# Key and query splits stored by the front, and per-pair near scores of the sample on three column tiles, in a hybrid attention, RG-LRU and HGRN2 layer

## The chip, the cores and the metric

One core of a Trainium2 chip runs the whole program in one launch. The metric is the device time of that launch in microseconds (us). Engines are named as in the profile: PE is the matmul engine (PEld its weight loads), DVE the vector engine, ACT the scalar engine, POOL GpSimd, SP the engine whose queue issues every DMA here.

## The reference, cut to what matters

One layer is applied to a prompt of 2048 positions and to a sample group of 8 sequences with 8 new tokens each, all in f32. After an RMSNorm the input is multiplied by `w_in` (1024 x 4608); the columns feed three head groups, whose gated outputs are multiplied by `w_out`, added to the input and normed.

- Group A (6 heads of 64) is dilated attention. For the prompt each query looks at keys at distance up to 128, at every 4th key up to 512 and at every 16th up to 2048; the three branches are merged by their softmax denominators:

```
scores = einsum('bthd,btnhd->bthn', q, kg) * dh ** -0.5
p = exp(scores - max); o = einsum('bthn,btnhd->bthd', p, vg) / sum(p)
out = sum_over_branches(softmax(lse) * o) * silu(g_A)
```

- For the sample the same three branches run over a cache of 2048 keys per sequence and the 8 new ones.
- Group B is a gated linear recurrence (RG-LRU) after a convolution, group C a chunked matrix recurrence (HGRN2).

Products that matter for precision are made of a high and a low part of each operand: x_hi is x rounded to fp32r, x_lo = x - x_hi, and the kernel adds two or three products of such parts.

## The kernel before, in words

The program has two blocks, with a barrier of all engines between them.

**front** (L266 to L1295) makes the projections. `front_schedule` (L155) returns one list of steps; every engine walks the same list and does its part of each step, so the list sets the order on each queue. A step `("p", ci, g)` is the product of one group of 128 columns with one of five column blocks of the tokens (512, 384, 384, 384, 448 wide; the last holds the 64 sample tokens): 24 matmuls into one of three PSUM banks. PE may start product i when product i - 3 has been read (`bank_free`, L1195). `FORDER` has the column groups: 6 for group B, then 3 of keys ("k"), then for each of 6 HGRN heads f, c and one of q0, q1, q2, a0, a1, a2. From there on each product is cut into a half step `"e"` and a half step `"p"`, and after each half a few steps of the HGRN recurrence run.

- Keys (ACT, L716 to L726): ACT copies the bank into `kf`, sorted by position modulo 4 ("by class"), and SP stores the whole of one key group, 128 rows of 8448 bytes, to `zf` in DRAM after its fifth product (L439). A step `"k"` turns `kf` with PE, copies on DVE and stores `k_win_prompt`.
- Queries (ACT, L708): the bank goes by class to `stage[0]`, and SP stores it to `zf` in pieces of 384 bytes (L430).
- SP walks the same list: the store of a product is issued at the next `"p"` step (`before`, L473 on).

**attend_project** (L1496 on) has the attention over the prompt and, interleaved in its first part, the products of the values and the sample's HGRN part; then the output product with the sample's attention between its steps. `attend_schedule` (L1401) returns its list.

- Each head has 32 units `"u"`. In a unit PE makes the scores of 128 queries against up to 512 keys as two matmuls (L2495 with `khi`, L2496 with `klo`) into one of three banks; the moving operand is `qst`, which holds query_hi in partitions 0 to 63 and query_lo in 64 to 127, with the key parts on both halves. DVE adds a mask and takes the row minimum (L2267), ACT takes the exponential (L2115). Later steps `"t"` turn four blocks of probabilities (L2563), copy them out of PSUM (L1634 on ACT, L1636 on DVE), and `"o"` multiplies them with the values (L2586). The `"t"` of head h begin 11 units into head h + 1. Before the first of them POOL scales all probabilities of the head in ten operations (L2021), when the branch weights are there.
- The split of keys and queries: raw keys and queries come from `zf` in 4 parts per head (two of keys, two of queries), twice each, for both partition halves (L1799, 8 DMAs of 256 KB per head). ACT rounds each part (L2072, step `"s"`), DVE subtracts (L2252 for keys, L2256 for queries, step `"sd"`), and for queries ACT copies the result into tile order as `qn` (L2077, step `"se"`). `khi`, `klo` have two buffers; `qst` and `qn` have one, so the last query part of a head is made at units 4, 6 and 8 of that head, the rest at units 12 to 26 of the head before.
- PE waits for the key split at the first unit of a head and for `q_near` at units 0 and 16 (L2484 on).

The sample's attention (steps `"sr"`, `"ss"`, `"sk"`, `"sc"`, `"sx"`, `"sn"`, `"sm"`, `"so"`, `"sb"`, one sequence b at a time) stands between the half tiles `"pp"` of the output product, each of which is 27 matmuls of 512 columns (L49 to L51). In `"sk"` PE turns the 512 near keys for three head pairs (L2451), and makes the near scores of all 6 heads as three accumulating products of 512 columns (L2456): `qbd` holds, for each pair, the 48 query rows of all heads with zeros in the rows of the other pairs, so output rows are 48 and each product adds one pair. The scores of the 8 new keys (L2462) and of the far keys (L2468) go to the same bank. The probabilities are then turned (L2611, L2612, L2616), and `"so"` multiplies with the values on three column tiles, 16 rows in each (L2630).

Of the kernel before, what the change touches and what calls it, by code (L numbers as in the profile page):

```python
# [110 lines left out]
FCOL = {"q": 0, "k": 384, "a": 1152, "x": 1536, "g": 1920, "c": 2304, "f": 3072}  # L111
ZROW = {"q": ZQ, "k": ZK, "a": ZGA, "c": ZQC, "f": ZFC}
# [153 lines left out]
def front(nc, sem, io, con, zf, zt, mab, mt):  # L266
# [7 lines left out]
    with ExitStack() as ctx:  # L274
        end = ROOM + 4 * FREE

        def sb(name, shape, dt=F32):
# [68 lines left out]
                 "fs_store", "st_store", "const", "held")  # L346
# [13 lines left out]
        stages, stored, z_count, kinds = {}, [0] * NR, {}, {}  # L360
        for s in made:
            kind = kinds[s] = "t" if s[0] == "t" else FORDER[s[1]][0]
            if s[0] == "t" or kind in "qa":
                r = 0 if s[0] == "p" else (len(stages) + (s[1] == 2)) % NR
                stages[s] = r, stored[r]
                stored[r] += 2 if kind == "q" and s[2] == NFG - 1 else 1
# [3 lines left out]
        gate_stores = [max(stages[("t", 1, j)][1] + 1 for j in range(XTILES) if stages[("t", 1, j)][0] == r) for r in range(NR)]  # L370
        by_class = lambda t: t.rearrange("p (g i) -> p g i", g=NC)
# [24 lines left out]
        def _(sp):  # L396
# [14 lines left out]
            def store(s):  # L411
# [12 lines left out]
                if kind == "q":  # L424
                    r = stages[s][0]
                    m = min(n, SEQ - t0)
                    rows = slice((ZQ + c) * P, (ZQ + c + 1) * P)
                    sp.wait_ge(S["z_out"], BASE + z_count[s])
                    dst = by_class(zf[rows, 0:SEQ])[:, :, t0 // NC:(t0 + m) // NC]
                    sp.dma_start(dst, by_class(stage[r][:, :m])).then_inc(z_store[r], 16)  # L430
                    if m < n:
                        sp.dma_start(zf[rows, SEQ:T], stage[r][:, m:n]).then_inc(z_store[r], 16)
# [40 lines left out]
            before = None  # L473
            for s in sched:
                kind, a, b = s
                if kind == "r" and a + NX < XTILES:
# [165 lines left out]
        def _(act):  # L642
# [39 lines left out]
            def out(s):  # L682
# [20 lines left out]
                if kind in "qa":  # L703
# [3 lines left out]
                    if kind == "q":  # L707
                        ins = A(by_class(stage[r][:, :m]), in_turn(src[:, :m]), ACT.Copy)  # L708
# [6 lines left out]
                elif kind == "k":  # L715
# [7 lines left out]
                    ins = A(by_class(kf[c % 2][:, 0:SEQ])[:, :, t0 // NC:(t0 + m) // NC], in_turn(src[:, :m]), ACT.Copy)  # L723
                    if m < n:
                        ins = A(kf[c % 2][:, SEQ:T], src[:, m:n], ACT.Copy)
# [2024 lines left out]
```

## Time and profile before

| | |
|---|---|
| runs | 1743.97, 1744.19, 1745.74 us; median 1744.19 |
| the profiled execution | 1739.62 us, of which the trace spans 1737.9 |
| PE busy | 1606.0 us, 92% |
| DVE, ACT, POOL busy | 1012.0, 844.6, 628.4 us |
| DMA | 162.69 MB, mean 94 GB/s |

The front takes the first 1079 us or so of the span, the attention over the prompt ends near 1420, the rest is the output product with the sample's attention. A time in the rows below is counted from the start of the span. A PE row's duration is modelled and overlaps with the next; the distance from one start to the next is what an instruction takes in a row of them. "Idle before" and the releaser name what an engine waited for.

### The profile page before, as it was taken

How to read it: one execution, taken by the hardware profiler on the slowest of the kernel's cores; microseconds unless marked ns; L12 is line 12 of the kernel's file. 1: busy time of each engine (PE TensorE's matmuls, PEld its weight loads, DVE VectorE, ACT ScalarE, POOL GpSimd, SP SyncE). 2: the span in 40 equal slices, each digit the busy share in tenths (PEclk: the TensorE clock that was granted, in tenths of full speed). 3: DMA queues.
4: the chain of work that ended last, by engine and by line, in shares of the span. 5: the costliest groups of instructions: out<-in, count | busy, mean ns of one | idle time of the engine just before them, and what ended most of it. 6: DMA issues, size and time to landing. Idle time of an engine off the chain costs nothing. (4 is left out here: it accounts for less than half of the span.)

```text
span 1737.9 us, 38458 instructions
## 1 busy us (share of the span) xinstructions
PE 1606.0 (92%) x15345; PEld 1343.2 (77%) x15345; DVE 1012.0 (58%) x2044; ACT 844.6 (49%) x1620; POOL 628.4 (36%) x745
## 2 busy tenths in 40 slices
PE   6999997999999999999999998798888988999998
PEld 5988986989888888888787877785666666767775
DVE  3437655322366777677776764348776556565552
ACT  4427874211355555666667772545777631111120
POOL 1002220200366766666666663114444621212110
PEclk9999998999999999999999999897999889999999
DMA  6311011113212121121212112437651175676651
GB/s 209 108 50 40 21 44 56 57 58 125 76 30 65 30 63 29 42 55 32 66 27 64 32 38 74 121 90 173 169 134 50 62 223 166 195 236 186 225 168 52
DMA packets 182703, 162.69 MB, mean 94 GB/s; under 512 B 65571, under 2 KB 169022, under 8 KB 182142
## 3 DMA queue, kind: packets, MB, share of 16 engines
q1 hardware_dynamic: 182526, 160.24, 31.2%
q8 instruction: 122, 2.00, 0.5%
q14 instruction: 55, 0.45, 0.1%
HBM read 116.89 MB, written 46.55 MB: 94 GB/s over the span
## 5 line engine op out<-in xcount | busy, mean ns | idle before, releaser
L49 PE MATMUL f_bank<-c_ht,c_whi 128*128 128x384 f32 (+1 forms) x864 | 321.1, 372 | 5.7 <-DVE c_wlo L866 5.7
L51 PE MATMUL f_bank<-c_ht,c_wlo 128*128 128x384 f32 (+1 forms) x864 | 303.3, 351 | 0.0
L50 PE MATMUL f_bank<-c_ht,c_whi 128*128 128x384 f32 (+1 forms) x864 | 302.7, 350 | 0.0
L815 ACT ACTIVATE f_scr<-f_scr 128x384 f32<-128x384 f32 (+1 forms) x210 | 114.0, 543 | 205.8 <-POOL f_scr L595 205.7
L1016 DVE TENSOR_TENSOR f_scr<-f_scr 128x192 f32<-128x192 f32 (+1 forms) x210 | 102.7, 490 | 138.9 <-ACT f_scr L815 138.7
L49 PEld LDWEIGHTS f_bank<-c_ht,c_whi 128*128 128x128 f32 x864 | 162.9, 189 | 21.3 <-DVE c_wlo L866 6.5
L50 PEld LDWEIGHTS f_bank<-c_ht,c_whi 128*128 128x128 f32 x864 | 163.3, 189 | 9.7 <-issue 1.1
L51 PEld LDWEIGHTS f_bank<-c_ht,c_wlo 128*128 128x128 f32 x864 | 162.9, 189 | 9.3
L594 POOL TENSOR_TENSOR f_scr<-f_scr 128x192 f32<-128x192 f32 (+1 forms) x210 | 134.8, 642 | 40.4 <-PE f_tps L1191 37.7
L1007 DVE COPY_PREDICATED f_scr<-f_scr,f_tps 128x384 f32<-128x384 int32 (+1 forms) x210 | 130.3, 621 | 18.7 <-PE f_tps L1191 9.7
L49 PE MATMUL a_s<-a_whi,a_mhi 128*128 128x512 f32 (+1 forms) x306 | 123.5, 404 | 4.7 <-DVE a_y L2426 4.7
L50 PE MATMUL a_s<-a_wlo,a_mhi 128*128 128x512 f32 (+1 forms) x306 | 120.5, 394 | 0.0
L620 POOL TENSOR_SCALAR f_scr<-f_scr,c_lbl 128x384 f32<-128x384 f32 (+1 forms) x30 | 43.3, 1443 | 211.3 <-ACT f_scr L781 211.3
L1191 PEld LDWEIGHTS f_tps<-f_scr 128*32 128x32 f32 (+1 forms) x5184 | 74.2, 112 | 41.4 <-issue 30.0
L1191 PE MATMUL f_tps<-f_scr 128*32 128x32 f32 (+1 forms) x5184 | 95.4, 200 | 4.1 <-DVE f_scr L1016 4.1
L2040 POOL TENSOR_TENSOR a_small<-a_small,c_mhalf 128x1 f32<-128x1 f32 (+1 forms) x17 | 9.2, 544 | 241.5 <-DVE a_small L2430 241.5
L49 PE MATMUL f_bank<-c_whi,c_ht 128*128 128x384 f32 x256 | 90.4, 353 | 3.7 <-DVE c_wlo L870 3.7
L51 PE MATMUL f_bank<-c_whi,c_ht 128*128 128x384 f32 x256 | 86.5, 338 | 0.0
L50 PE MATMUL f_bank<-c_wlo,c_ht 128*128 128x384 f32 x256 | 86.4, 338 | 0.0
L49 PE MATMUL f_bank<-c_htail,c_whi 128*128 128x448 f32 x216 | 84.3, 390 | 0.0
L51 PE MATMUL a_s<-a_whi,a_mlo_a 128*128 128x512 f32 (+1 forms) x204 | 80.3, 394 | 0.0
L51 PE MATMUL f_bank<-c_htail,c_wlo 128*128 128x448 f32 x216 | 79.4, 368 | 0.0
(400 smaller groups left out, 3901.2 us busy)
## 6 DMA issues: line engine op xcount, KB each, us to landing
f_wraw<-in_w_in SPq DMA_DIRECT2D x27, 512.0 KB, 4.0
a_raw<-zf SPq DMA_DIRECT2D x48, 256.0 KB, 4.0
a_k<-in_ck SPq DMA_DIRECT2D x48, 192.0 KB, 4.5
a_v<-in_cv SPq DMA_DIRECT2D x48, 192.0 KB
f_scr<-in_xp SPq DMA_DIRECT2D x16, 512.0 KB, 4.3
a_x<-in_xp SPq DMA_DIRECT2D x16, 512.0 KB, 4.8
out_y_prompt<-a_y SPq DMA_DIRECT2D x16, 512.0 KB, 2.9
zt<-f_stage SPq DMA_DIRECT2D x38, 192.0 KB, 1.8
```

The source lines that it names most:

```text
L49: nc.tensor.matmul(out, w_hi, m_hi, start=start, stop=False)
L50: nc.tensor.matmul(out, w_hi, m_lo, start=False, stop=False)
L51: return nc.tensor.matmul(out, w_lo, m_hi, start=False, stop=stop)
L594: G.tensor_tensor(d[:, :, hs:], b[:, :, hs:], r, ALU.subtract)
L620: G.tensor_scalar(key[:, :n], key[:, :n], lbl[:, 1, h:h + 1], None, ALU.mult).then_inc(S["gated"], 1)
L815: A(lev[i % 3][:, :n], lev[i % 3][:, :n], ACT.Exp).then_inc(S["expd"], 1)
L1007: V.copy_predicated(attn[:, :n].rearrange("p (j t) -> p j t", t=P), m.bitcast(I32).unsqueeze(1).to_broadcast([P, nt, P]), lp[x % 2][:, :n] ...
L1016: V.tensor_tensor(e[:, :, hs:], e[:, :, hs:], q[:, :, hs:], ALU.mult).then_inc(S["xlev"], 1)
L1191: mm = nc.tensor.matmul(lp[x % 2][k0:k0 + w, queries], left[:, keys], right[:, queries], start=True, stop=True)
L2040: G.tensor_tensor(s[:, 2:3], s[:, 1:2], con["mhalf"][:rows_of(n), 0:1], ALU.pow).then_inc(Z["rstd"], 1)
```

## The change

In the front, keys and queries are split there and stored as high and low part, by class, in a new DRAM tensor `zs` (4 x 384 rows x 2048). ACT copies a key bank to `kf` as before and a second time, rounded, to `stage[0]`; DVE subtracts that from the bank into `stage[1]`; SP stores both after each key product, and only the 64 sample columns of `kf` go to `zf`. For queries ACT writes the rounded part to `stage[0]`; SP stores it at the next `"e"` step; when it has landed DVE overwrites it with the difference, at the `"e"` step after that, and SP stores again. A bank of keys or queries is free for PE only when its low part has been made.

In the attention all of `"s"`, `"sd"` and `"se"` is gone. SP loads the parts, ready-made, per head: 6 DMAs of 512 KB with rows of 8192 bytes (`"lk"`), at unit 19 of head 0 for head 1 and at unit 2 of head h for head h + 1. `qst` and `qn` have two buffers. `qn` is copied on ACT for heads 0 and 1 (step `"qa"`) and on POOL for the others (step `"qn"`, after units 12 and 22 of the head before). PE waits for `qn` at units 4 and 20 of a head, which first need it. The loads of values and gates that followed a split step follow unit 18 of head 1 (`"lv"`).

In the sample's attention the score rows become 96: pair pr has rows 32 pr to 32 pr + 15 and 16 rows of zeros. Near and new scores are one product per pair on a column tile of its own, with no accumulation, all three near ones after the turning of all keys, the far scores and the next query's product. The far scores' weights have 96 columns instead of 48; near probabilities are turned with 96 columns instead of 48, far ones with 80; DVE takes the turned far part in three operations instead of one.

```diff
@@ front: stages
+            elif kind == "k":
+                key_stages[s] = list(stored)
+                stored = [n + 1 for n in stored]
@@ front, SP
+                def split(row, r):
+                    dst = by_class(zs[row + c * P:row + (c + 1) * P, :])[:, :, t0 // NC:(t0 + m) // NC]
+                    sp.dma_start(dst, by_class(stage[r][:, :m])).then_inc(z_store[r], 16)
+                if kind == "q" and part:
+                    sp.wait_ge(S["q_low"], BASE + NFG * c + s[2] + 1)
+                    split(SQL, 0)
+                elif kind == "q":
                     sp.wait_ge(S["z_out"], BASE + z_count[s])
+                    split(SQH, 0)
...
-                elif kind == "k" and s[2] == NFG - 1:
+                elif kind == "k":
                     sp.wait_ge(S["z_out"], BASE + z_count[s])
-                    sp.dma_start(zf[(ZK + c) * P:(ZK + c + 1) * P, :], kf[c % 2]).then_inc(kf_store[c % 2], 16)
+                    split(SKH, 0)
+                    sp.wait_ge(S["k_low"], BASE + NFG * c + s[2] + 1)
+                    split(SKL, 1)
...
@@ front, ACT, keys
+                    if key_stages[s][0]:
+                        act.wait_ge(z_store[0], BASE + 16 * key_stages[s][0])
+                    if NFG * c + s[2]:
+                        act.wait_ge(S["k_low"], BASE + NFG * c + s[2])
+                    A(by_class(s_high[:, :m]), in_turn(src[:, :m]), ACT.Copy).then_inc(S["z_out"], 1)
@@ front, DVE
+            def key_low(s):
...
+                dve.wait_ge(S["z_out"], BASE + z_count[s])
+                dve.wait_ge(z_store[1], BASE + 16 * key_stages[s][1])
+                V.tensor_tensor(by_class(s_low[:, :n]), in_turn(bank[place[s] % 3][:, :n]), by_class(s_high[:, :n]),
+                                ALU.subtract).then_inc(S["k_low"], 1)
+            def query_low(s):
...
+                dve.wait_ge(z_store[0], BASE + 16 * (stages[s][1] + 1 + (s[2] == NFG - 1)))
+                V.tensor_tensor(by_class(s_high[:, :n]), in_turn(bank[place[s] % 3][:, :n]), by_class(s_high[:, :n]),
+                                ALU.subtract).then_inc(S["q_low"], 1)
@@ front, PE, bank_free
+                elif kind in "kq":
+                    pe.wait_ge(S["k_low" if kind == "k" else "q_low"], BASE + NFG * FORDER[s[1]][1] + s[2] + 1)
@@ attend_schedule
-    for step in ("ha", "va", "vb", "s0", "hb", "va", "hp", "s1", "ht", "hc", "vb", "s2", "hd", "va", "vb", "hx", "s3", "va"):
...
+    for step in ("ha", "va", "vb", "hb", "va", "hp", "qa", "ht", "hc", "vb", "hd", "va", "vb", "hx", "va"):
+        order.append(halves.pop(0) if step[0] == "v" else (step, 0))
+    order.append(("qa", 1))
...
-            order += [(step, 4 * (h + 1) + part) for part, (first, steps) in enumerate(((12, ("s", "sd")), (16, ("s", "sd")), (22, ("s", "sd", "se"))))
-                      for at, step in enumerate(steps) if k == first + 2 * at]
-        if h and k in (4, 6, 8):
-            order.append((("s", "sd", "se")[k // 2 - 2], 4 * h + 3))
+            order += {2: [("lk", h + 1)], 12: [("qn", 2 * h + 2)], 18: [("lv", 1)] * (h == 1), 22: [("qn", 2 * h + 3)]}.get(k, [])
@@ attend_project, SP
+            def load_split(h):
+                p, rows = h % 2, lambda part: zs[part + h * HD:part + (h + 1) * HD, :]
+                for d, part in enumerate((SQH, SQL)):
+                    sp.dma_start(qst[p][d * HD:(d + 1) * HD, :].bitcast(F32), rows(part)).then_inc(q_in[p], 16)
+                for dst, part in ((khi[p], SKH), (klo[p], SKL)):
+                    for d in range(2):
+                        sp.dma_start(dst[d * HD:(d + 1) * HD, :].bitcast(F32), rows(part)).then_inc(k_in[p], 16)
@@ attend_project, POOL
+                elif kind == "qn":
+                    h = n // 2
+                    pool.wait_ge(q_in[h % 2], BASE + 32 * (h // 2 + 1))
+                    pool.wait_ge(S["scores"], BASE + PER * (h - 1))
+                    tiles, src = near_queries(n)
+                    G.tensor_copy(tiles, src).then_inc(S["q_near"], 1)
@@ attend_project, PE, sample
             def score(b, pr):
-                read(pe, f"K{pr}", b)
-                mm = nc.tensor.matmul(scr[:R, 0:NEAR], qbd[:, b, pr * R:(pr + 1) * R], kt[:, pr, :], start=(pr == 0), stop=(pr == 2))
+                rows = slice(pr * QR, (pr + 1) * QR)
+                mm = nc.tensor.matmul(scr[rows, 0:NEAR], qbd[:, b, rows], kt[:, pr, :], start=True, stop=True)
...
                     new_scores(n)
-                    score(n, 0)
                     turn_keys(n, 2)
                     far_scores(n)
-                    score(n, 1)
                     if n + 1 < NB:
                         query(n + 1)
-                    score(n, 2)
+                    read(pe, "K1", n)
+                    read(pe, "K2", n)
+                    for pr in range(3):
+                        score(n, pr)
```

## Rows read from the trace of the kernel before

**Rows 1.** The page: the span, and the granted PE clock in 40 slices

```profile
span 1737.9 us, 38458 instructions
...
PEclk9999998999999999999999999897999889999999
```

**Rows 2.** PE's waits from 1083 to 1190 us: us in total, times, longest

```profile
PE a_t L2475 <- DVE a_h_qc L2274: 3.8, 1, 3.8
PE a_s L2495 <- issue: 2.6, 1, 2.6
PE a_t L2475 <- ACT a_h_kdt L2109: 2.2, 1, 2.2
PE a_t L2510 <- ACT a_h_kd L2102: 1.9, 1, 1.9
PE a_s L2495 <- ACT a_qn L2077: 1.8, 1, 1.8
```

**Rows 3.** PE's waits from 1186 to 1376 us

```profile
PE a_s L2495 <- DVE a_sn L2267: 20.4, 8, 6.4
PE a_t L2563 <- ACT a_pt L1634: 6.3, 15, 0.7
```

**Rows 4.** Windows: busy PE, PEld, DVE, ACT, POOL; PEclk, DMA share, GB/s

```profile
1186.00:1200.00 14.00, 7.56 (x48) 6.49 (x49) 11.45 (x16) 5.95 (x17) 11.77 (x5) 0.74 0.51 120
1200.00:1222.00 22.00, 21.32 (x187) 15.92 (x185) 15.57 (x58) 17.46 (x50) 0.00 (x0) 0.94 0.98 227
1222.00:1262.60 40.60, 34.37 (x297) 25.80 (x297) 29.55 (x88) 29.67 (x86) 18.69 (x10) 0.96 0.51 146
...
1303.00:1345.40 42.40, 35.96 (x297) 26.93 (x297) 29.61 (x88) 29.69 (x86) 18.68 (x10) 0.92 0.20 51
1345.40:1376.00 30.60, 28.64 (x242) 21.92 (x240) 19.36 (x61) 24.04 (x72) 17.70 (x10) 0.94 0.07 17
```

**Rows 5.** Timelines of DVE and POOL in heads 1 and 2 of the attention

```profile
1190.24 8.61 DVE L2252 TENSOR_TENSOR a_klo<-a_raw,a_khi 128x1024 fp32r<-128x1024 f32 x1
...
1233.88 4.32 DVE L2252 TENSOR_TENSOR a_klo<-a_raw,a_khi 128x1024 fp32r<-128x1024 f32 x1 [0.15 <-ACT a_khi L2072]
...
1241.74 1.23 DVE L2252 TENSOR_TENSOR a_klo<-a_raw,a_khi 128x1024 fp32r<-128x1024 f32 x1 [0.77 <-ACT a_khi L2072]
...
1233.51 7.31 POOL L2021 TENSOR_TENSOR a_pf<-a_pf,a_wt 128x2048 f32<-128x2048 f32 x2
```

**Rows 6.** Timeline of PE, one sequence of the sample's attention

```profile
1463.71 1.06 PE L2456 MATMUL a_o<-a_kt,a_qbd 128*48 128x512 f32 x2
1464.70 0.66 PE L2451 MATMUL a_t<-c_ident,a_k 128*128 128x128 f32 x4
1465.29 0.71 PE L2468 MATMUL a_o<-a_selm,a_far_rows 128*48 128x16 f32 x12
...
1475.05 0.44 PE L2611 MATMUL a_t<-c_ident,a_prob 48*128 48x48 f32 x4
1475.34 0.20 PE L2612 MATMUL a_t<-c_ident,a_prob 48*8 48x48 f32 x1
...
1482.50 2.70 PE L2630 MATMUL a_x<-a_v,a_ptt 128*16 128x128 f32 x66
1485.13 0.50 PE L49 MATMUL a_s<-a_whi,a_mhi 128*128 128x512 f32 x1
```

**Rows 7.** PE's waits in the output stage: the far scores of the sample

```profile
PE a_o L2468 <- DVE a_far_rows L2377: 2.3, 4, 0.7
```

**Rows 8.** DMA issues: count, KB each, median us to landing

```profile
zf<-f_stage SPq DMA_DIRECT2D x21, 192.0 KB, 2.1
zf<-f_scr SPq DMA_DIRECT2D x3, 1056.0 KB, 3.9
```

**Rows 9.** Timeline of ACT: the first bank of key groups 1 and 2

```profile
396.73 0.60 ACT L723 ACTIVATE f_scr<-f_bank 128x512 f32<-128x512 f32 x1 [4.88 <-PE f_bank L51]
...
421.56 0.60 ACT L723 ACTIVATE f_scr<-f_bank 128x512 f32<-128x512 f32 x1 [4.88 <-PE f_bank L51]
```

More of the change, by code:

```diff
@@ L263, in front_schedule, with front @@
     return order
[L266 removed]
+def front(nc, sem, io, con, zf, zt, zs, mab, mt):
     NC3 = AW // P
@@ L370, in front @@
         gate_stores = [max(stages[("t", 1, j)][1] + 1 for j in range(XTILES) if stages[("t", 1, j)][0] == r) for r in range(NR)]
+        key_lows = max(used[1] for used in key_stages.values()) + 1
+        s_high, s_low = (stage[r][:].bitcast(F32R) for r in range(NR))
         by_class = lambda t: t.rearrange("p (g i) -> p g i", g=NC)
@@ L471, in _ @@
             load_x(4)
-            before = None
+            before = queries = None
             for s in sched:
                 kind, a, b = s
-                if kind == "r" and a + NX < XTILES:
+                if kind == "e":
+                    if queries is not None:
+                        store(queries, 1)
+                        queries = None
+                    elif before is not None and kinds[before] == "q":
+                        queries, before = before, None
+                        store(queries)
+                elif kind == "r" and a + NX < XTILES:
                     sp.wait_ge(S["normed"], BASE + a + 1)
@@ L1061, in output @@
                 V.tensor_tensor(o, o, w, ALU.mult).then_inc(S["out"], 1)
-            last = None
+            last = queries = None
             for s in sched:
@@ L1066, in _ @@
                 if s in place or kind == "e":
+                    if kind == "e" and queries is not None:
+                        query_low(queries)
+                        queries = None
                     if last is not None and kinds[last] == "a":
                         silu(last)
+                    elif last is not None and kinds[last] == "k":
+                        key_low(last)
+                    elif last is not None and kinds[last] == "q":
+                        queries = last
                     last = s if s in place else None
@@ L1578, in attend_project @@
         store = [sem(f"a_store{p}") for p in range(2)]
-        S = {n: sem("a_" + n) for n in ("iota", "mask", "hi", "split", "q_near", "scores", "shifted", "exped", "own",
+        S = {n: sem("a_" + n) for n in ("iota", "mask", "q_first", "q_near", "scores", "shifted", "exped", "own",
                                         "masks", "far_out", "far_in", "back_out", "back_in", "apart", "expw", "weights", "scaled", "turned", "copied_a", "copied_v", "used", "final",
@@ L1671, in attend_project, with near_queries @@
         hw = lambda h: slice(h * P, (h + 1) * P)
+        def near_queries(n):
+            p, c = n // 2 % 2, slice(n % 2 * CLS // 2, (n % 2 + 1) * CLS // 2)
+            tiles = qn[p][:].rearrange("p (j g u) -> p g j u", g=NC, u=QR)[:, :, c.start // QR:c.stop // QR, :]
+            return tiles, cls(qst[p][:])[:, :, c].rearrange("p g (j u) -> p g j u", u=QR)
         def tile_out(eng, j):
@@ L2244, in _ @@
             for kind, n in order:
[L2245 to L2258 removed]
+                if kind == "u":
                     h, i, far, m = units[n]
```

192 lines of the change are left out of this document (86 added, 106 removed).

## The prediction

> **What bounds the kernel now.** The page first: the granted PE clock [rows 1] is 9 in nearly every slice of the front, dips where the attention starts and ends, and PE is busy 92% of the span. So PE is the bound, and work taken from DVE or ACT helps only where PE waits for them. I then listed PE's waits stage by stage. In the front they are few. In the attention they are not: 12.3 us in five waits up to the first units of head 1 [rows 2], and from 1186 to 1376 us 20.4 us in eight waits for DVE's masked scores, the longest 6.4 us, beside 6.3 us in fifteen for ACT's copies of turned probabilities [rows 3]. The windows by head show PE busy 34.4 of 40.6 us, DVE 29.6, ACT 29.7 [rows 4]: no engine is full, they are coupled through three score banks. The timelines of DVE tell what PE waits for: a key split, L2252, stands in DVE's queue ahead of the next masked score. Alone it takes 1.23 us, but 4.32 us in head 2 while POOL scales probabilities for 7.31 us, and 8.61 us in head 1 [rows 5]. So it is held up while POOL works. These waits also cost clock: granted 0.74 in the window of the 6.4 us wait, 0.92 to 0.96 in later heads [rows 4]. In the output stage PE is packed; what counts there is what PE itself executes.
>
> **The start of the attention, -5 us.** Four waits, 9.7 us without the one marked "issue" [rows 2]. The 3.8 us wait is for `h_qc`, queued on DVE behind one key split: 1.2 us goes, the mask building ahead of it stays. The 1.8 us wait is for the first `qn`, itself the end of load, round, subtract and copy: it goes, since units now wait for `qn` only from unit 4. The 1.9 us (L2102 on ACT, behind the `qn` copy) and the 2.2 us (ACT's `h_kdt`, behind exponentials that waited for a DVE split) keep about half, as the exponentials and a `qa` copy remain (1024 columns, at most the 1.23 us of DVE's subtraction of that size [rows 5]). That is 5 of 9.7; bounds 2 and 8 (all but the masks, and some clock). First parts of head 0: 3 MB by DMA; seven half tiles of value products cover them. Without that cover the price would be 3 MB at 227 GB/s [rows 4], 14 us.
>
> **The first units of head 1, -2.5 us.** The 2.6 us wait marked "issue" [rows 2] ends with ACT's `qn` copy. It goes if head 1's load, issued at unit 19 of head 0 some 18 us earlier, lands in time: 14 us at the rate above. Bounds 0 and -2.6.
>
> **Heads 1 to 5, -28 us.** (a) The eight waits of 20.4 us [rows 3] are all behind splits; I keep 1.5 us for other lateness: -19. (b) Of the waits for ACT's copies those right after a split, about 2 us of 6.3, follow from it: -2. (c) Clock: a window of T us at granted c loses (1 - c) T against full speed: 3.6 + 1.3 + 1.6 + 1.6 + 3.4 + 1.8 = 13.3 us over the windows from 1186 to 1376 [rows 4] (the fourth is a head like the third). Shorter waits should not lower it, but not all low clock lies behind splits: I take 9, bounds 0 and 13.3. (d) New work: eight `qn` copies of 1024 elements on POOL. The nearest row is 7.31 us for two operations of 2048 and 1536 elements with two inputs [rows 5], 2.1 us per 1024; a copy costs at most that, 4 us per head on an engine busy 18.7 of 40.6 us [rows 4]. They come behind the ten scalings and are wanted only in the next head, so they cost nothing; should POOL be late, the scalings of the next head are next in its queue. (e) At a faster pace something new shows: ACT has 29.7 less six dropped copies of about 1 us, 24 us of work, in some 34: +2. Sum -19 - 2 - 9 + 2 = -28. Bounds: -15 (half the waits come back elsewhere, no clock) and -37. SP's DMA issues in a head fall from 8 to 6; per head 3 MB instead of 2 must come in 34 us, 92 GB/s, beside what the windows show (51 to 227). The load for head h + 1 is issued at unit 2 of head h, behind nothing but the store of results of head h - 2, and SP's wait on scores there is met already.
>
> **The sample's near scores, -6 us.** A near score takes 0.99 us from start to start (1463.71 to 1464.70 [rows 6]), 2.97 for the three. How three column tiles run side by side is shown by L2630: 66 instructions of 128 columns in 2.63 us, 40 ns each [rows 6]. A near score is two passes (x2) of 512 columns, so one pass is 0.43 to 0.49 us (the first from 1.06 us modelled for two less a tail of 0.2), or 107 ns and more per 128 columns: the tiles overlap 2.7-fold. The three scores should take 2.97 / 2.7 = 1.1 us, 1.87 less. In four of eight sequences, though, PE waits for DVE's far rows (2.3 us in four waits [rows 7]), and the first score, 0.99 us, stood ahead of that wait. Taken away, it lengthens the wait: these save 0.88 us. The last key copy can hide behind the far scores and the next query's product; in the last sequence behind the far scores alone. 4 x 1.87 + 4 x 0.88 = 11. Against that, per sequence: five near transposes with 96 columns instead of 48, 73 ns each now (1475.05 to 1475.34 for four), and six far ones with 80; four of 128 columns take 147 ns each (1464.70 to 1465.29), so by interpolation +44 and +30 ns each, 0.4 us; twelve far scores (0.71 us [rows 6]) with 96 weight columns, +0.2 us. 8 x 0.6 = 5. Net -6; bounds -11 (nothing added shows) and +5 (no overlap at all). DVE's two extra small operations lie beside PE's half tiles.
> The Trainium skill (TensorE: Matmul & The Clock Gate, Measured speedup vs the span model) gives 2.38-fold for three column tiles at 512 columns; by that the three take 1.25 us, 1.2 us less gain over the stage. The Trainium skill (TensorEngine Tiling (Array Packing), Key Properties) says that changing the tiling mode drains the array, which speaks against two more excursions per sequence; L2630's 2.63 us end with such a change and hold no more than one.
>
> **The front, +1.5 us.** Thirty subtractions on DVE, about 0.5 us each (384 columns at L2252's 1.23 us for 1024 [rows 5]), fifteen more ACT copies of 0.5 (0.60 for 512 columns [rows 9]), and instead of 3 row stores 30 piece stores. None stands on PE's queue; PE now waits for the low part, two products later than it is made. Per key product (24.8 us for five, 5.0 each [rows 9]) the chain is: ACT copy 0.5, issue 0.4, store landed 2.1 (the like store of queries [rows 8]), next ACT copy; 3.2 us with semaphores, under 5.0. Where step `"k"` holds SP and DVE, two free banks (10 us) cover it. For queries the extra subtraction sits between DVE's steps of the recurrence, fifteen times; I let a fifth of it, 0.1 us, reach PE. +1.5; bounds 0 and +6.
>
> **Sum.** -5 - 2.5 - 28 - 6 + 1.5 = -40 us. The profiled execution took 1739.6 us (span 1737.9 and 1.7 around it), so 1699.6 for one like it; the median of the runs stands 4.6 us above the profiled one, and by that the forecast is 1704 us.
>
> **The rivals.**
> 1. *The waits move.* With splits gone PE reaches the next link sooner, POOL's scalings (18.7 us per head, busy 17.7 of the last 30.6 [rows 4]) or ACT's copies, waits there, and the clock stays as it is. For: the POOL chain must be done from unit 4 to unit 26. Against: at 1.05 us per unit that is 22 us against 15. Heads give 15 instead of 28: 1717 us. Chance 0.17.
> 2. *Column tiles don't overlap* for f32 with 512 columns and different moving rows. Against: L2630 also reads different rows per tile. Stage +5 instead of -6: 1715 us. Chance 0.09.
> 3. *The loads are late.* Around head 2's start the DMA engines are already 98% busy at 227 GB/s [rows 4], and 1 MB more per head is asked of them. Two heads each wait 5 us: 1714 us. Chance 0.08.
> 4. *Slower than before: key stores pace the front.* Key parts leave in pieces of 384 bytes. A row store moves 1056 KB in 3.9 us, a piece store 192 KB in 2.1 [rows 8], so pieces are dear, and there are two per product now, with weights and k_win stores beside them. It decides once a store takes more than 3.8 us from issue to landing (5.0 less copy, issue, semaphores). To outweigh 40 us over fifteen products with 10 us of slack it needs 3.3 us more per product, a landing above 7.1 us; at 7.5 us it gives 15 x 3.7 - 10 = 46 us: 1750 us. Against: the same store of queries lands in 2.1. Chance 0.05.
> The Trainium skill (DMA: Bandwidth & Descriptors, Specifications) asks for pieces of at least 512 bytes, below which an engine reads, modifies and writes; that is the rule behind this rival, and the rows agree in direction.
> 5. *It does not do what it says*: splits gone, but the waits on banks were PE's own order, so nothing moves. The 8.61 and 4.32 us rows speak against it: inside the others.
>
> **Numbers.** Forecast case 0.61, at 1704. The range takes in rivals 1 to 3 and most of the forecast's bounds: low 1690 (waits and clock of the heads back in full, the sample at -11), high 1722 (rival 1 with the front at +6). A measurement of this kernel tells 0.2%, 3.5 us, from no change. Faster by more: all but rival 4 and a thin edge, 0.94; within: 0.01; slower: 0.05.
>
> **What the profile after would show.** Right: no L2252, L2256, L2072; PE's waits for `a_sn` under 4 us in the heads; PEclk 0.98 or more there; head period 33 to 35 us instead of 40.6; `"k"` period still 5.0 us; the three near scores within 1.3 us; far-score waits near 6 us instead of 2.3. Wrong: a new wait of PE on POOL's `a_pf` or on the loads of `khi` and `qst`; score starts 0.43 us apart on different tiles; landings of the `zs` stores above 3.8 us.

## The result and the profile after

The changed kernel took 1689.12 us (median of 4 runs, 1685.58 to 1692.14), the kernel before 1744.97 beside it: ratio 0.968, 95% interval 0.966 to 0.970, so 56 us faster. The forecast was 1704 us and the range ended at 1690. The direction was right, and so was the largest term; the gain was larger than forecast, 0.9 us beyond the end of the range (two repeats of the change, below, gave 1687.66 and 1687.98).

The profiled execution took 1692.14 us. Cut at the same places (ACT's copy of the first key bank, PE's first value product, head 1's first unit, the first output product), the two traces give these windows, before and then after (length, busy PE, PEld, DVE, ACT, POOL, then granted clock, DMA share, GB/s):

```profile
0.00:396.73 396.73, 360.95 (x1888) 330.68 (x1889) 186.31 (x321) 195.20 (x306) 56.73 (x80) 0.98 0.22 73
396.73:1079.22 682.49, 653.72 (x9363) 564.00 (x9362) 441.11 (x859) 392.23 (x659) 389.70 (x541) 1.00 0.18 51
1079.22:1166.64 87.42, 75.08 (x490) 70.16 (x491) 37.28 (x113) 44.46 (x106) 15.35 (x30) 0.92 0.39 106
1166.64:1421.31 254.67, 215.89 (x1710) 155.97 (x1710) 176.38 (x471) 163.08 (x443) 114.21 (x64) 0.87 0.49 128
1421.31:1737.90 316.59, 300.40 (x1898) 222.38 (x1897) 170.92 (x280) 49.59 (x107) 52.43 (x31) 0.98 0.57 181
```

```profile
0.00:398.72 398.72, 362.87 (x1888) 332.27 (x1889) 189.14 (x326) 197.28 (x311) 56.68 (x80) 0.97 0.23 75
398.72:1080.69 681.97, 656.44 (x9363) 566.34 (x9362) 450.89 (x884) 396.82 (x669) 389.87 (x541) 0.99 0.21 58
1080.69:1159.74 79.05, 74.66 (x491) 70.44 (x491) 28.62 (x101) 35.47 (x94) 15.37 (x30) 0.92 0.55 135
1159.74:1376.23 216.49, 201.64 (x1711) 149.19 (x1710) 135.36 (x459) 144.77 (x424) 114.58 (x72) 0.91 0.70 173
1376.23:1690.40 314.17, 293.28 (x1898) 227.60 (x1897) 172.18 (x296) 49.58 (x107) 52.38 (x32) 0.96 0.57 182
```

Read the lengths: the heads gave 38.2 us, the start of the attention 8.4, the output stage 2.4, the front's changed part 0.5. Ahead of the key products, where both kernels are the same, this execution was 2.0 us longer; together 47.5, the difference of the two spans (1737.9 and 1690.4).

Inside the heads the picture of [rows 4] is gone. Heads 1 to 4, from first unit to first unit, and the stretch from head 5 to the output product:

```profile
1159.74:1201.78 42.04, 39.09 (x223) 25.18 (x221) 28.60 (x94) 25.17 (x78) 24.10 (x16) 0.76 0.96 219
1201.78:1233.85 32.07, 31.65 (x295) 24.53 (x294) 20.29 (x83) 24.55 (x80) 18.69 (x12) 1.00 1.06 276
1233.85:1265.57 31.72, 31.59 (x296) 24.53 (x295) 19.74 (x83) 25.08 (x81) 18.69 (x12) 1.00 0.98 217
1265.57:1297.65 32.08, 31.66 (x295) 24.53 (x294) 20.36 (x83) 24.64 (x80) 18.68 (x12) 1.00 0.53 117
1297.65:1376.23 78.58, 67.65 (x612) 50.42 (x611) 46.38 (x118) 45.33 (x113) 34.40 (x20) 0.89 0.36 111
```

In heads 2 to 4 PE is busy 31.6 of 32 us at full clock: nothing is left for any engine to hold up, though the DMA share is 1.06 and 0.98 in two of them. The waits of PE from 1160 to 1330 us, all there are, which answer to [rows 3]:

```profile
PE a_x L2594 <- DVE a_exch L2230: 1.1, 1, 1.1
PE a_t L2613 <- ACT a_pt L1677: 0.7, 2, 0.3
PE a_x L2602 <- DVE a_exch L2230: 0.6, 1, 0.6
PE a_t L2577 <- DVE a_h_s L2347: 0.6, 1, 0.6
PE a_t L2613 <- POOL a_pf L2082: 0.3, 1, 0.3
PE a_s L2545 <- DVE a_sn L2306: 0.3, 1, 0.3
```

In the output stage the wait of [rows 7] has grown from 2.3 to 6.2 us, as forecast:

```profile
PE a_o L2513 <- DVE a_far_rows L2418: 6.2, 4, 1.7
```

### The profile page after: what moved, and what is told of

It is laid out like the page before. It is cut to its first block and busy times, and to the rows that moved or that the text cites. A ratio compares the mean times of both kernels' runs of the same rounds, so it can differ in the third digit from the quotient of the medians.

```text
span 1690.4 us, 38531 instructions
## 1 busy us (share of the span) xinstructions
PE 1588.9 (94%) x15345; PEld 1345.8 (80%) x15345; DVE 976.2 (58%) x2066; ACT 823.9 (49%) x1603; POOL 628.9 (37%) x754
## 5 line engine op out<-in xcount | busy, mean ns | idle before, releaser
L49 PE MATMUL f_bank<-c_whi,c_ht 128*128 128x384 f32 x256 | 92.3, 360 | 2.2 <-DVE c_wlo L897 2.2
L51 PE MATMUL f_bank<-c_whi,c_ht 128*128 128x384 f32 x256 | 88.2, 344 | 0.0
L49 PE MATMUL f_bank<-c_htail,c_whi 128*128 128x448 f32 x216 | 84.3, 390 | 0.0
L50 PE MATMUL f_bank<-c_htail,c_whi 128*128 128x448 f32 x216 | 79.3, 367 | 0.0
```

The lines of the kernel that those rows point to most:

```text
L49: nc.tensor.matmul(out, w_hi, m_hi, start=start, stop=False)
L50: nc.tensor.matmul(out, w_hi, m_lo, start=False, stop=False)
L51: return nc.tensor.matmul(out, w_lo, m_hi, start=False, stop=stop)
```

## The experiments

Each kernel is the changed one with one edit, unless it is called the kernel before. They ran in groups. The changed kernel itself ran beside the old sample part, near scores first and the last head's copies (1687.66 us, and 1745.12 for the kernel before). The other kernels had only the kernel before beside them (1741.98 for the four of the second table below, 1744.54 for the chain, the two kernels made from the one before, and the last kernel), so there a distance to 1687.66 is uncertain by some us. I also compare the length of the changed stage, from the profile, which leaves out the differences ahead of the key products.

**The change again**, and both kernels a second time.

> The change itself, again. Theory: the medians moved by 55.9 us (1744.97 to 1689.12), the two profiled executions by 47.5 (1739.62 to 1692.14), because the profiled one of before was the fastest seen of its kernel and that of after the slowest of its own. A median from 1686 to 1691 us, ratio to before 0.966 to 0.970. Rival: the change is worth what the two traces show, 48 us: a median of 1695 or more.

Measured: 1687.66 us against 1745.12, ratio 0.968 (0.966 to 0.970). The profile has the heads at 216.5 us and the output stage at 314.1, as in the first one, but head 1 begins 5.2 us earlier, mostly ahead of the key products. A third profile of it, and two more of the kernel before:

> The kernel before itself, profiled once more. The medians differ by 55 to 57 us, the stages of the two traces by 49.5. Theory: part of the waits before was a matter of chance (where a split met one of POOL's instructions), and the one profiled execution of before fell well: in other executions the heads, from head 1's first unit to the output product, take 257 us or more instead of 254.7, with the rest of the stages the same within 1 us. Rival: the heads are the same within 1 us in every execution and the spread lies ahead of the key products, where both kernels are the same.

> As b_again1, one more execution: theory, heads at 257 us or more in at least one of the two; rival, 254 to 255.5 in both.

> The changed kernel, a third profiled execution: by either account its heads take 216.2 to 216.8 us, since PE waits for nothing there; what spread it has lies ahead of the key products.

Stage lengths, cut as above, in us:

| | before, three profiles | after, three profiles |
|---|---|---|
| up to the keys | 396.7, 398.6, 397.3 | 398.7, 394.1, 394.9 |
| keys to attention | 682.5, 683.0, 683.0 | 682.0, 682.3, 682.5 |
| start of attention | 87.4, 89.0, 90.6 | 79.1, 78.1, 77.7 |
| heads | 254.7, 254.8, 252.8 | 216.5, 216.5, 216.8 |
| output | 316.6, 316.0, 316.0 | 314.2, 314.1, 314.2 |

The theory fell: the heads of the kernel before were never at 257. The rival holds nearly as it was put (the heads spread by 2.0 us, not 1), but it was not whole: the start of the attention spreads too, by 3.2 us, and the trace of the prediction had its shortest. Medians beside these: 1687.98 against 1742.48, ratio 0.969 (0.967 to 0.972).

**What in the heads made the 38 us.** Three kernels put back part of the removed work as idle work in a scratch tile (960 columns, 1.15 us on DVE), in the places where it stood.

```diff
+        if h and (k in (6,) or h + 1 < NH and k in (14, 18, 24)):
+            order.append(("dd", h))
...
+                elif kind == "dd":
+                    V.tensor_tensor(dum[:].rearrange("p (a w) -> p a w", a=2), twice(fmask), twice(fmask), ALU.subtract).then_inc(S["dum"], 1)
```

(`twice` reads 480 columns two times.) The second kernel has `(2,)` and `(26, 28, 30)` there. The third has six copies on ACT instead, and a fourth makes the near queries on ACT:

```diff
+        if h and (k in (4, 8) or h + 1 < NH and k in (12, 16, 22, 26)):
+            order.append(("dd", h))
...
+                    A(dum[:].rearrange("p (a w) -> p a w", a=2), twice(fmask), ACT.Copy).then_inc(S["dum"], 1)
```

```diff
-                    G.tensor_copy(tiles, src).then_inc(S["q_near"], 1)
...
+                    A(tiles, src, ACT.Copy).then_inc(S["q_near"], 1)
```

> The changed kernel with one idle subtraction of 960 columns on DVE (into a scratch tile) after units 6, 14, 18 and 24 of the heads, where the splits stood before; nothing on ACT. Theory: DVE's splits behind POOL's scaling were the whole stall. The one at 18, and the one at 14, stretch to 4 us and more, PE waits for the masked scores return (8 to 16 us in heads 1 to 4), the waits for turned probabilities return with them though ACT has no work added (3 us or more), and the clock falls to 0.92 to 0.96: 15 to 28 us slower than the change, 1704 to 1717 us. Rival: the splits mattered through what PE waited for in data (key parts not ready), or through ACT's share: under 5 us slower.

> The same four subtractions, but after units 2, 26, 28 and 30, where POOL does not scale. Theory: each takes about 1.2 us and hides behind the three score banks: at most 4 us slower than the change, 1689 to 1693 us, no PE wait for masked scores over 1 us, clock 1.00. Rival: it is DVE's amount of work that counts, not where it stands: as slow as the run with the splits in their old places, 15 us or more.

> The changed kernel with six idle copies of 960 columns on ACT per head, after units 4, 8, 12, 16, 22 and 26, where its rounding and tile-order copies stood before. Theory: ACT has 24.6 us of work in 32 and six more of 1 us bring it to 30.6; PE waits for turned probabilities come back in part (1 to 3 us over the heads), none for masked scores over 0.7 us: 2 to 8 us slower than the change, 1691 to 1697 us. Rival: half of the stall before was ACT's: 15 us slower or more.

> The changed kernel with the eight near-query copies of heads 2 to 5 on ACT instead of POOL. Theory: POOL's copies are free (POOL is idle for 13 us per head behind them) and ACT has room for two of 1.05 us per head: within 2 us of the change, 1687 to 1691 us. Rival: that they went to POOL is what lets PE run without a wait: 5 us slower or more.

Measured, as medians and as the length of the heads (216.5 in the change):

| | median | heads | head 1, 2, 3, 4 |
|---|---|---|---|
| subtractions in the old places | 1707.75 | 233.7 | 51.0, 34.3, 34.1, 34.3 |
| the same at units 2, 26, 28, 30 | 1702.50 | 230.2 | 42.8, 38.4, 34.1, 34.6 |
| ACT copies in the old places | 1687.44 | 213.6 | 41.4, 32.2, 31.9, 32.2 |
| near queries on ACT | 1689.63 | 216.1 | 41.4, 33.1, 31.7, 32.1 |

ACT's copies alone cost nothing, where 2 to 8 us were expected: with 29 us of work in 32 (its busy time with the six copies) ACT still holds nobody up. Nor does it matter where the near queries are copied. Four subtractions are worth 17 us, as expected, but 9 of them in head 1, where one took 8.59 us. In heads 2 to 4 they took 1.15 to 3.06 us, not the 4 us and more that were expected (the splits of before took up to 4.70 there), and the clock stayed at 1.00. The second run misses its expectation: moved away from POOL's scaling each took 1.15 to 1.18 us (a row below, from the end of head 2), and yet they cost 13.7 us in the heads. That is near the rival's figure, so the amount of DVE's work has a price of its own in those places. They fell beside the head's change, where DVE's short chain of branch weights stands (PE waited 4.4 us in four for `a_exch`), and head 2 ran at a clock of 0.87:

```profile
1235.03 1.15 DVE L2318 TENSOR_TENSOR a_dum<-a_fmask 128x960 f32<-128x960 f32 x1
```

Neither part alone reaches the 7.8 to 9.6 us that heads 2 to 4 had lost. So the whole chain was put back, with its order:

```diff
+        if h:
+            order += [(("ds", "dd", "de")[step], h) for first, steps in ((4, 3), (12, 2), (16, 2), (22, 3)) for step in range(steps)
+                      if k == first + 2 * step and (first == 4 or h + 1 < NH)]
```

> The changed kernel with the whole of the old split work as idle work in its old places: ACT copies after units 4, 12, 16, 22, DVE subtracts in place two units later when that copy is done, ACT copies the result after units 8 and 26. Theory A (the chain and its meetings with POOL): four subtractions alone cost 17 us (2.3 per head in heads 2 to 4), six copies alone nothing, but the subtraction's wait for ACT's copy holds DVE's queue as well and shifts where it meets POOL; together 25 to 40 us slower than the change, 1713 to 1728 us, with waits for masked scores of 15 us or more and a clock of 0.92 to 0.96 in the heads. Rival B: the parts add, 15 to 20 us slower, 1703 to 1708 us; what is left of the change's gain in the heads is then not the engines' work, but the buffers and loads.

Measured: 1727.04 us, 39 slower than the change, heads 249.9 us against 254.7 before. Heads 1 to 4:

```profile
1161.73:1212.38 50.65, 41.72 (x223) 26.58 (x221) 40.08 (x98) 29.64 (x82) 26.24 (x16) 0.73 0.98 220
1212.38:1253.51 41.13, 35.67 (x296) 26.53 (x294) 28.79 (x86) 28.99 (x86) 21.48 (x12) 0.92 0.65 167
1253.51:1293.99 40.48, 35.58 (x296) 26.67 (x294) 28.64 (x87) 29.82 (x86) 21.48 (x12) 0.92 0.79 172
1293.99:1334.28 40.29, 34.94 (x296) 26.28 (x294) 28.87 (x86) 29.10 (x86) 21.49 (x12) 0.92 0.41 90
```

That is nearly the kernel before again, waits (17.4 us in eight for masked scores) and low clock included, with the loads and buffers of the change. So 33 of the 38 us in the heads are the removed work of the engines, in its order, and PE waited for none of the larger loads; the other 5 us stay open. Here the subtractions that meet the scaling late took 3.69 to 4.48 us in heads 2 to 4, as the splits had. How one subtraction meets POOL, in this kernel, DVE and then POOL:

```profile
1186.58 8.58 DVE L2324 TENSOR_TENSOR a_dum<-a_fmask,a_dum 128x960 f32<-128x960 f32 x1
...
1229.88 4.48 DVE L2324 TENSOR_TENSOR a_dum<-a_fmask,a_dum 128x960 f32<-128x960 f32 x1
```

```profile
1187.83 3.60 POOL L2091 TENSOR_TENSOR a_pf<-a_pf,a_wt 128x2048 f32<-128x2048 f32 x1
1191.40 2.75 POOL L2091 TENSOR_TENSOR a_pf<-a_pf,a_wt 128x1536 f32<-128x1536 f32 x1
...
1229.74 3.60 POOL L2091 TENSOR_TENSOR a_pf<-a_pf,a_wt 128x2048 f32<-128x2048 f32 x1
```

The subtraction of 1229.88 came 0.14 us after a POOL instruction of 3.60 us began and ended 1.02 us after that one's end: it waited for the whole instruction. The one of 1186.58 began beside an earlier POOL instruction, let the two shown pass as well, and ended 1.01 us after the second (1194.15).

**POOL taken away from the kernel before.** The scaling of the probabilities is cut to one element per operation, so the branch weights are missing in the prompt's attention.

```diff
-                        G.tensor_tensor(p, p, by_row.unsqueeze(2).to_broadcast([P, ms, w]), ALU.mult).then_inc(S["scaled"], 1)
+                        G.tensor_tensor(p[:, 0:1, 0:1], p[:, 0:1, 0:1], by_row[:, 0:1].unsqueeze(2), ALU.mult).then_inc(S["scaled"], 1)
```

> The kernel BEFORE with POOL's scaling of the probabilities cut down to one element per operation (the branch weights are left out of the result); the splits stay where they were. Theory: a subtraction on DVE that arrives while a POOL instruction runs waits for its end, and only that made splits long; without POOL's work all take 1.2 to 1.4 us, PE's waits for masked scores fall from 20.4 us to under 5, the clock in heads 2 to 4 comes to 0.98 or more and their period from 40 to 42 us to 33 to 35: 25 to 35 us faster than before, 1710 to 1720 us. Rival: DVE's and ACT's amount of work is what PE waits for: period 38 us or more, under 12 us faster.

Measured: 1704.17 us against 1744.54, ratio 0.977 (0.975 to 0.980), 40 us faster, more than the 25 to 35 that the theory gave. All 19 splits from 1157 us on took 1.22 to 1.37 us; where one had taken 8.61:

```profile
1193.96 1.23 DVE L2252 TENSOR_TENSOR a_klo<-a_raw,a_khi 128x1024 fp32r<-128x1024 f32 x1
```

```profile
1212.47:1247.39 34.92, 32.71 (x295) 24.46 (x294) 24.77 (x86) 29.26 (x86) 1.47 (x10) 1.00 0.71 194
```

```profile
PE a_t L2563 <- ACT a_pt L1634: 4.7, 13, 0.6
...
PE a_s L2495 <- DVE a_sn L2267: 0.3, 1, 0.3
```

With every split still there the clock is 1.00, the wait for masked scores is 0.3 us, and the heads take 217.0 us (part of that is the last head, where POOL's scaling is waited for). A head is still 2.8 us longer than in the change (34.9 against 32.1, 1.8 of it idle): that is what the splits and copies cost without POOL's scaling. The rest, 5 to 7 us per head and the low clock of heads 2 to 4, needs both.

**Could the splits have stayed, in other places?**

```diff
-            order += [(step, 4 * (h + 1) + part) for part, (first, steps) in enumerate(((12, ("s", "sd")), (16, ("s", "sd")), (22, ("s", "sd", "se"))))
+            order += [(step, 4 * (h + 1) + part) for part, (first, steps) in enumerate(((3, ("s", "sd")), (25, ("s", "sd")), (27, ("s", "sd", "se"))))
...
-        if h and k in (4, 6, 8):
-            order.append((("s", "sd", "se")[k // 2 - 2], 4 * h + 3))
+        if h and k in (0, 2, 4):
+            order.append((("s", "sd", "se")[k // 2], 4 * h + 3))
```

> The kernel BEFORE with its splits moved, none removed: the last query part of a head rounded after unit 0 and subtracted after unit 2, the first key part for the next head after 3 and 5, the second key part after 25 and 27, the first query part after 27 and 29, so that none stands where POOL scales. Theory: splits of 1.2 us, period of heads 2 to 4 at 34 to 37 us (the idle subtractions in such places cost 2.4 to 6 us per head): 14 to 24 us faster than before, 1720 to 1730 us. Rival: the work itself is the price wherever it stands: within 8 us of before.

Measured: 1764.02 us against 1744.54, ratio 1.011 (1.008 to 1.014): slower by 20, where the theory gave 14 to 24 faster. The splits were short (1.22 to 1.55 us), but a new wait took their place:

```profile
PE a_s L2495 <- ACT a_qn L2077: 18.3, 4, 4.6
PE a_t L2563 <- DVE a_h_s L2308: 14.4, 1, 14.4
```

The tile-order copy now came after unit 31, and unit 0 of the next head reads it. The second wait is POOL again, with another of DVE's operations: a product for the sample's state, both inputs in SBUF, which takes 0.69 us alone. It began at 1186.55 beside one POOL instruction of the scaling, and four more passed before it ended, 0.55 us after the last of them (1197.98), DVE and then POOL:

```profile
1186.55 11.98 DVE L2305 TENSOR_TENSOR a_h_s<-a_h_s,a_h_gl 128x512 f32<-128x512 f32 x1
```

```profile
1191.67 6.31 POOL L2021 TENSOR_TENSOR a_pf<-a_pf,a_wt 128x2048 f32<-128x2048 f32 x2
```

In the kernel before the longest of these six products took 1.99 us. So to move the splits moved the meeting. The heads took 273.2 us at a clock of 0.81. A placement that avoids both waits was not tried.

**The sample's near scores.** The sample's part as before, in the changed kernel:

```diff
-    R, USED = 3 * QR, 2 * QR + 2 * NT
+    R = NH * NT
...
+                    score(n, 0)
                     turn_keys(n, 2)
                     far_scores(n)
+                    score(n, 1)
```

> The changed kernel with the sample's attention as before (48 score rows, near scores as three accumulating products, the first of them ahead of the far scores). Theory, from the two traces: the output stage was 2.4 us shorter with the change, because the waits for the far rows grew from 2.3 to 6.2 us and the clock in the stage fell from 0.98 to 0.96; so about 2 to 4 us slower than the change, 1691 to 1694 us, far-row waits of some 2.3 us and a clock of 0.98 in the stage. Rival, the term as forecast: 6 us slower, 1695 us or more.

Measured: 1690.21 us (the expectation began at 1691), an output stage of 316.6 us against 314.1, far-row waits of 2.3 us, clock 0.98. The term is worth 2.4 us. Where the rest of it went is in two timelines of PE in the changed kernel, a sequence without and one with the wait:

```profile
1446.47 1.11 PE L2513 MATMUL a_o<-a_selm,a_far_rows 128*96 128x16 f32 x12
1447.52 0.91 PE L2491 MATMUL a_t<-a_qtok,a_selq 64*128 64x384 f32 x2
1448.36 1.06 PE L2501 MATMUL a_o<-a_kt,a_qbd 128*32 128x512 f32 x6
1449.35 0.30 PE L2687 MATMUL a_t<-c_ident,a_orow 96*128 96x96 f32 x1
```

```profile
1477.92 1.38 PE L2501 MATMUL a_o<-a_kt,a_qbd 128*32 128x512 f32 x6
1479.24 0.42 PE L2687 MATMUL a_t<-c_ident,a_orow 96*128 96x96 f32 x1
1479.37 0.77 PE L49 MATMUL a_s<-a_whi,a_mhi 128*128 128x512 f32 x1
1479.94 0.63 PE L50 MATMUL a_s<-a_wlo,a_mhi 128*128 128x512 f32 x1
1480.36 0.63 PE L51 MATMUL a_s<-a_whi,a_mlo_a 128*128 128x512 f32 x1
```

The three near scores take 0.99 us (1448.36 to 1449.35) where one took that in [rows 6]: threefold, not 2.7-fold. The twelve far ones take 1.05 instead of 0.56. In the second timeline the scores take 1.32 us and the matmuls of the next half tile stand 0.43 us apart, against 0.23 without the wait: the granted clock from 1479.4 to 1482.0 us is 0.51, the lower level (1.2 GHz), behind a wait of 1.69 us. Behind the longest wait before, 0.70 us, they stood 0.23 apart. So the wait costs twice.

```diff
+                    near_keys(n, 1)
...
-                    V.tensor_copy(kt[:, 1, :], bank("K1", n)[:]).then_inc(Z["kt_v"], 1)
...
                     turn_keys(n, 2)
-                    far_scores(n)
                     if n + 1 < NB:
                         query(n + 1)
...
                     for pr in range(3):
                         score(n, pr)
+                    far_scores(n)
```

> The changed kernel with two things altered in the sample's key step: ACT copies the second key bank too (DVE did), and PE makes the three near scores before the far ones, not after. Theory: PE's waits for the far rows (6.2 us in four) go, since 1.9 us of other work now stands ahead of them, and with them the low clock of the half tile behind each; the stage's clock comes to 0.98 or more; 8 to 12 us faster than the change, 1677 to 1681 us. Rival: the wait only moves, to the copies of the keys on ACT or to the probabilities that PE turns next, and the clock dips there as well: 1687 to 1689 us.

Measured: 1685.23 us (1682.24 to 1688.12), only 2.4 under the change, where 8 to 12 were expected; the medians alone hardly tell the two apart. The stage took 308.4 us in the profile, 5.8 less. The far-row wait is gone, but a new one took 3.7 us, for the query selection, which DVE makes behind its far sum:

```profile
PE a_t L2487 <- DVE a_selq L2274: 3.7, 3, 1.4
```

**The last head.** Two splits of output weights (1024 columns each, 7.67 us together beside POOL) kept a copy of probabilities from PE for 5.9 us (4.5 before the change).

```diff
-        owner = ["v" if t % 4 == 3 else "a" for t in range(len(groups))]
+        owner = ["v" if t % 4 == 3 and t < len(groups) - 16 else "a" for t in range(len(groups))]
```

> The changed kernel with the last 16 copies of turned probabilities all on ACT; in the change every fourth is on DVE, where one stood behind two splits of output weights that took 7.67 us beside POOL's scaling, and PE waited 5.9 us for it. Theory: that wait goes to under 1 us, 4 to 7 us faster than the change, 1682 to 1685 us. Rival: ACT, which rounds the output weights at 1.05 us each in between, becomes the pace (0.60 and 1.05 us per group against 1.17 now), or the DMA wait of 2.4 us behind it grows: 1687 to 1690 us.

Measured: 1686.10 us, the last stretch 78.5 us instead of 78.7. The rival was right: PE waited 5.4 us for ACT's copies instead. Then both stages together, each in another form:

```diff
+                    if n + 1 < NB:
+                        dve.wait_ge(Z["q_spread"], BASE + n + 1)
+                        select(n + 1)
                     dve.wait_ge(Z["product"], BASE + n + 1)
...
-        if 4 <= n < 4 + KM:
+        if 8 <= n < 8 + KM:
```

> The changed kernel with (a) near scores ahead of the far ones and all three key copies on ACT, as in e_near_first, and the selection for the next query made on DVE ahead of the sum over the far keys, since e_near_first left 3.7 us of waits for it; (b) the splits of the output weights begun four groups later, after POOL's last scaling. Theory: (a) takes the output stage from 308.4 us in e_near_first to 303 to 306; (b) the stretch from the first unit of head 5 to the output product from 78.6 to 72 to 75 us. Together 9 to 16 us faster than the change, 1672 to 1679 us. Rival for (a): the wait moves to the far rows or the keys and the stage stays at 308; for (b): the weights are late for the output product, or another of DVE's operations meets POOL, and the stretch stays at 78 us.

Measured: **1676.30 us** (1674.99 to 1678.45), ratio to before 0.961 (0.960 to 0.963), 11 us under the change and the fastest of all. The output stage is 303.7 us at a clock of 0.98 with PE busy 288.2, against 314.2 at 0.96 and 293.3; the last stretch 76.9 us, short of the 72 to 75 expected, as PE still waits 5.6 us for DVE's copies of probabilities there.

```profile
1372.83:1676.50 303.67, 288.21 (x1898) 224.34 (x1897) 167.65 (x288) 53.49 (x115) 52.72 (x32) 0.98 0.58 185
```

## Why the prediction missed

**Heads, -28 forecast, -38.2 measured: the step that failed.** The mechanism was right, shown by putting it back (33 of the 38 us) and by taking POOL's scaling away. What failed is how much of the coupled loss I let go with the splits: three of the four parts were mis-sized. (a) The waits for masked scores went from 20.4 to 0.3 us, -20.1 for -19. (b) Of the waits for ACT's copies I kept two thirds as independent; 0.7 of 6.3 are left, -5.6 for -2. In heads 1 to 4 they stand at 0.7 us with ACT's idle copies alone, 2.5 with the subtractions alone and 3.9 with the chain; without POOL's scaling, where PE hardly waits for masked scores, they are still 4.7. So they came from the splits together with their copies, not only from the long splits. (c) The clock: I took 9 of 13.3 us as a hedge and named full recovery the bound. It recovered fully in heads 2 to 4. In the whole stretch, for the same matmuls, PE's busy time fell from 215.9 to 201.6 us, 14.3. (e) The new coupling, +2, is not there: six ACT copies more still cost nothing. PE's idle time fell from 38.8 to 14.9 us, 23.9, where (a), (b) and (e) gave 19; idle and busy together are the 38.2.

**The start of the attention, -7.5 forecast, -8.4 measured.** By the means of three profiles it is -10.7, since the trace of the prediction had the shortest start; that is just beyond my bounds for its two terms (8 and 2.6). No run puts its parts back one by one, so its causes are read from the traces. The waits for `qn` are gone, both of them; `h_qc` is now waited for 1.8 us (3.8 before), `h_kdt` 1.8 (2.2), `h_kd` 0.8 (1.9):

```profile
PE a_t L2520 <- ACT a_h_kdt L2161: 1.8, 1, 1.8
PE a_t L2520 <- DVE a_h_qc L2313: 1.8, 1, 1.8
PE a_t L2560 <- ACT a_h_kd L2154: 0.8, 1, 0.8
```

**Near scores, -6 forecast, -2.4 measured.** What PE executes shrank about as forecast. Per sequence at full clock the three scores take 1.98 us less (1.87 forecast) and the wider pieces 0.57 more (0.6 forecast), otherwise spread: 0.49 for the far scores (0.2), 0.08 for five near transposes (0.22), nothing to be seen for the far ones (0.18). That is 11 us in eight sequences; in the last kernel above, with the far-row wait gone, PE is busy 12.2 us less than before (288.2 against 300.4). What failed is the price of the far-row wait. I took its length rightly (near 6 us), but priced it at its length alone; in the change some 5 us of slow clock came with it (293.3 us busy against 288.2).

**Front, +1.5 forecast, -0.5 measured**, within the spread of 0.5 us: nothing. Rival 4, the store as pace, can be seen and is absorbed. The stores land in 2.4 us, but each waits behind others, and ACT waits for them up to 5.01 us; group 2 begins all the same 24.8 us after group 1:

```profile
398.72 0.60 ACT L746 ACTIVATE f_scr<-f_bank 128x512 f32<-128x512 f32 x1 [4.50 <-PE f_bank L51]
...
414.46 0.49 ACT L753 ACTIVATE f_stage<-f_bank 128x384 fp32r<-128x384 f32 x1 [5.01 <-DMA zs<-f_stage]
...
423.56 0.60 ACT L746 ACTIVATE f_scr<-f_bank 128x512 f32<-128x512 f32 x1 [2.82 <-PE f_bank L51]
```

**From a profile to the median.** I added the 4.6 us by which the profiled execution of before stood under its median. The changed kernel's own profiled execution stood 3.0 over its median, so profiles fell by 47.5 us and medians by 55.9. The mean of three profiles each is -52.4 (1739.6 to 1687.2 us of span): heads -37.5, start -10.7, output -2.0, the front's changed part -0.6, and -1.6 ahead of it, where nothing was changed. Against the forecast of -40 the heads gave 9.5 us more, the start 3.2 and the front 2.1, the near scores 4.0 less. The 3.5 us between -52.4 and the medians stay open.

**The rivals.** 1 (waits move to POOL or ACT) did not happen in heads 1 to 4: POOL's scaling was waited for 0.3 us (in the last head for 2.0, as before). 2 (no overlap) is wrong. 3 (late loads) is wrong although the rows are worse than feared: 12 loads each of `qst`, `khi` and `klo` landed in 7.0, 10.4 and 14.2 us, at a DMA share of 1.06 in head 2, and PE never waited for one. 5 is refuted by the chain put back: with the same buffers, 33 us returned.

## What to carry to other kernels

Work that was removed from the side engines' queues returned more here than the waits for it: add up all the waits it is an ancestor of, and the clock, before hedging any of them. Before a DVE operation with both inputs in SBUF is placed, look at what POOL runs at that moment and which other such operations would then meet POOL: a DVE operation of 0.7 to 1.2 us waited here for the rest of one POOL instruction or of several in a row, and so did everything queued behind it. And where an edit takes PE work from in front of a wait, move other work there in the same edit, since the wait cost its length here and then the slower clock behind it.

## What the runs showed that was not expected

A DVE operation with both inputs in SBUF and an instruction of POOL's scaling exclude each other, an instruction at a time. In the kernel before, the split of 4.32 us [rows 5] began 0.37 us into this first POOL instruction and ended 1.09 us after its end, and the second took 3.74 us where it takes 2.75 undisturbed (the POOL row of 1191.40 in the chain kernel above):

```profile
1233.51 3.60 POOL L2021 TENSOR_TENSOR a_pf<-a_pf,a_wt 128x2048 f32<-128x2048 f32 x1
...
1237.09 3.74 POOL L2021 TENSOR_TENSOR a_pf<-a_pf,a_wt 128x1536 f32<-128x1536 f32 x1
```

The masked scores (input in PSUM) took 0.42 us beside POOL as without it. The Trainium skill states this in SBUF — State Buffer, section SBUF: two separate sides: the shared port pair is an exclusive lock, held for a whole instruction, against a DVE operation with two SBUF inputs. The rows agree, and add that the waiting DVE operation does not always come next: in head 1 it let two more POOL instructions pass (8.58 and 8.61 us), and with the splits moved four (11.98 us). Had I read the 4.32 us by that rule, POOL would have stood in the forecast as the cause and not as a circumstance; that alone would not have changed its sum.
